# A second block's down projection as seven products with staggered rounds, and its up blocks as 256-column products

## The reference

```
u   = rms_norm(h, norm_mlp_pre)                    # 256 x 1024
hid = square(relu(u @ w_up))                       # 256 x 4096
m   = hid @ w_down                                 # w_down is 4096 x 1024
out = h + rms_norm(m, norm_mlp_post)
```

## Time and profile before

| what | value |
|---|---|
| median of three runs | 1020.5 us |
| the profiled execution, span from first to last instruction | 1018.8 us |
| PE busy | 1010.3 us, 99% of the span |
| DVE busy | 758.5 us, 74% |
| ACT busy | 556.8 us, 55% |
| POOL busy | 232.6 us, 23%; two one-column powers are all it does from 821 us to the end |
| granted TensorE clock, mean | 0.998 |

### The profile page before, as it was taken

The page is one execution under the profiler, slowest core; times in us unless marked ns, Lnnn a source line. Parts: engine busy times, 40 slices in busy tenths (PEclk is TensorE's granted clock), DMA queues, the critical chain, the costliest instruction groups (busy, mean ns, idle before and its releaser), DMA issues.

```text
span 1018.8 us, 14751 instructions
## 1 busy us (share of the span) xinstructions
PE 1010.3 (99%) x5688; PEld 851.1 (84%) x5688; DVE 758.5 (74%) x1208; ACT 556.8 (55%) x848; POOL 232.6 (23%) x322
## 2 busy tenths in 40 slices
PE   9999999999999999999999999999999999999997
PEld 6877788888888877788888888998888888888886
DVE  6997568788777887578787778888865457766665
ACT  6575566545556466656554556845544455334433
POOL 0572600000000272800000004019947620000000
PEclk9999999999999999999999999999999999999999
DMA  9641545555554351365554544553445556564541
GB/s 362 232 159 59 176 155 207 190 182 207 194 180 173 114 218 42 125 221 193 212 195 177 207 168 163 171 201 119 170 150 184 204 186 227 191 214 174 182 149 41
DMA packets 27894, 180.24 MB, mean 177 GB/s; under 512 B 3120, under 2 KB 3248, under 8 KB 7472
## 3 DMA queue, kind: packets, MB, share of 16 engines
q1 hardware_dynamic: 27824, 179.30, 49.5%
HBM read 178.24 MB, written 1.05 MB: 176 GB/s over the span
## 4 chain that ended last, share of the span: by engine, by line
PE 97%; DVE 1%; ACT 1%; DMA 0%; issue 0%; SPq 0%; DVEq 0%
PE pb L747 17%; PE pb L752 10%; PE pb L609 9%; PE pb L610 9%; PE pb L612 8%; PE pb L772 6%; PE pb L771 6%; PE pb L773 6%; PE pb L754 3%; PE pb L1017 2%; PE pb L970 2%; PE pb L673 1%; PE pb L672 1%; PE pb L674 1%; PE pb L709 1%; PE pb L985 1%
## 5 line engine op out<-in xcount | busy, mean ns | idle before, releaser
L1895 DVE TENSOR_TENSOR wlo<-raw,whi 128x2048 fp32r<-128x2048 f32 (+1 forms) x125 | 282.8, 2265 | 102.4 <-ACT whi L1374 102.2
L1374 ACT ACTIVATE whi<-raw 128x2048 fp32r<-128x2048 f32 x159 | 298.5, 1881 | 60.5 <-PE pb L612 34.6
L2772 POOL TENSOR_TENSOR wlo<-raw,whi 128x256 fp32r<-128x256 f32 x268 | 206.8, 810 | 318.9 <-ACT whi L1374 315.2
L747 PE MATMUL pb<-hb,whi 128*128 128x512 f32 x770 | 183.7, 389 | 0.0
L747 PEld LDWEIGHTS pb<-hb,whi 128*128 128x128 f32 x770 | 144.6, 188 | 30.4
L609 PE MATMUL pb<-whi,hb 128*128 128x512 f32 x336 | 134.2, 399 | 0.1
L610 PE MATMUL pb<-wlo,hb 128*128 128x512 f32 x336 | 130.9, 390 | 0.0
L612 PE MATMUL pb<-whi,hb 128*128 128x512 f32 x320 | 124.9, 390 | 0.0
L752 PEld LDWEIGHTS pb<-hb,wlo 128*128 128x128 f32 x880 | 112.8, 191 | 4.3
L752 PE MATMUL pb<-hb,wlo 128*128 128x256 f32 x880 | 114.2, 283 | 0.0
L772 PE MATMUL pb<-wlo,gh 128*128 128x512 f32 x280 | 109.2, 390 | 0.0
(11 more groups left out here) (404 smaller groups left out, 1558.8 us busy)
## 6 DMA issues: line engine op xcount, KB each, us to landing
raw<-wst SPq DMA_DIRECT2D x159, 1024.0 KB, 4.8
raw<-wst SPq DMA_DIRECT2D x10, 512.0 KB, 4.3
gb<-gains SPq DMA_DIRECT2D x3, 512.0 KB, 6.4
XN<-xt SPq DMA_DIRECT2D x2, 512.0 KB, 5.3
X<-x SPq DMA_DIRECT2D x1, 1024.0 KB, 12.1
out<-X SPq DMA_DIRECT2D x4, 256.0 KB, 2.0
PQ<-prm SPq DMA_DIRECT2D x1, 909.0 KB, 4.5
raw<-wst SPq DMA_DIRECT2D x2, 256.0 KB, 7.3
```

Source lines behind the costliest of these rows:

```text
L747: e.matmul(b[:, :], wh[:, k, s], hb2[:, k, :, :].rearrange("p i q -> p (i q)"), start=k == 0, stop=False)
L1374: e.activation(whi[:, split_slot(m), 0:w], raw[:, m % RAW, 0:w], ACT.Copy).then_inc(*hi(m))
L1895: e.tensor_tensor(wlo[:, split_slot(m), s], raw[:, m % RAW, s], whi[:, split_slot(m), s].bitcast(F32), ALU.subtract).then_inc(*lo_v(m))
L2772: g = e.tensor_tensor(wlo[:, split_slot(m), s], raw[:, m % RAW, s], whi[:, split_slot(m), s].bitcast(F32), ALU.subtract)
```

## The change

The down projection of every round is made of seven block products where there were eight, after Winograd's form of Strassen's method. The 256 tokens, the 256 hidden features and the 1024 output columns of a round are each cut in two, so that `hid` and `w_down` become 2 x 2 blocks. Products 1, 2 and 4 take blocks of `hid` and of `w_down` (with one exception: the block of product 4 is replaced by the sum that GpSimd leaves in `raw`); products 3, 5, 6 and 7 take sums of blocks. Each product is 3 matmuls (high and low parts) of 512 columns and has a PSUM bank of its own over all rounds, so a round has 21 matmuls where it had 24, and the output is put together from the seven banks once, at the end.

The sums are new work. GpSimd (`weight_sums`) makes three sums of w_down's blocks in `sums_at`, and a fourth in place in `raw`: four steps of 512 columns in pieces of 256, eight instructions. VectorE makes the sums of hidden blocks, `token_sums` (512 columns, in three instructions). All sums need high and low parts: ACT makes `shared_high` (1536 columns) and `tokens_high` (512), VectorE the low parts of 1024 columns and of `tokens_low`, GpSimd the low part of the last 512 columns in two pieces.

The up blocks are 24 matmuls of 256 columns each (`narrow_block`), which all add into the same 256 columns of one bank. ACT takes them out with relu (`evict`), and VectorE only squares them; the reduce over the two halves is gone. The first round's up blocks stay as they were.

The rounds are staggered: after round j's first up block TensorE takes products 3, 5, 6 and 7 of round j - 2, after its second up block products 1, 2 and 4 of round j - 1. The up tiles now alternate between two split buffers, even down tiles have a third, and odd ones one of their own; these and the sums lie in memory that earlier stages used.

```diff
+            def narrow_block(j, i):
+                m = ups[j]
+                wh, wl = (w.rearrange("p (k c) -> p k c", k=8) for w in parts(m))
+                s, b = slice(128 * i, 128 * i + 128), up_half(j, i)
+                q.wait_ge(*hi[m])
+                bank_free(up_bank(j, i))
+                for k in range(8):
+                    e.matmul(b, wh[:, k, s], hh[:, k, :], start=k == 0, stop=False)
+                    e.matmul(b, wh[:, k, s], hl[:, k, :], start=False, stop=False)
+                q.wait_ge(*lo_of(m)[m])
+                for k in range(8):
+                    mm = e.matmul(b, wl[:, k, s], hh[:, k, :], start=False, stop=k == 7)
+                mm.then_inc(*(used(m) if i else half_used(m)))
...
+            def quarter_products(j, *names):
...
+                for n in names:
+                    if n in (1, 2, 4):
+                        weights_ready(m)
+                        q.wait_ge(*gl_done[m])
+                    else:
+                        q.wait_ge(*tokens_lo[j])
+                    if n in (5, 6):
+                        q.wait_ge(*sums_lo[j])
+                    if n == 7:
+                        q.wait_ge(*sums_lo_g[j])
...
+                    o, (high, low, w_high, w_low) = PB[b][:, :], pair[n]
+                    e.matmul(o, high, w_high, start=j == 0, stop=False)
+                    e.matmul(o, high, w_low, start=False, stop=False)
+                    mm = e.matmul(o, low, w_high, start=False, stop=j == 15)
...
-                for j in range(16):
-                    b = 2 * (j % 2)
-                    if j:
-                        wide(tile_at[2, "up", j, 0], (b, b + 1), lp)
-                    else:
-                        wide_by_k(tile_at[2, "up", 0, 0], (0, 1), lp, [hh_done[("lp", 2), "column", k] for k in range(8)])
...
+                for j in range(1, 16):
+                    narrow_block(j, 0)
+                    free[up_bank(j, 0)] = ff_low[2, j, 0]
+                    if j > 1:
+                        quarter_products(j - 2, 3, 5, 6, 7)
+                    narrow_block(j, 1)
+                    free[up_bank(j, 1)] = ff_low[2, j, 1]
+                    quarter_products(j - 1, 1, 2, 4)
+                quarter_products(14, 3, 5, 6, 7)
+                quarter_products(15, 1, 2, 4, 6, 7, 5, 3)
...
+                def quarters_high(j):
+                    q.wait_ge(*summed_w[j])
+                    q.wait_ge(*used[slot_before(downs[j])])
+                    e.activation(parts(downs[j])[0], raw[:, downs[j] % RAW, :], ACT.Copy).then_inc(*hi(downs[j]))
+                def sums_high(j):
+                    q.wait_ge(*summed_w[j])
+                    q.wait_ge(*(used[downs[13]] if j == 15 else used[downs[j - 1]] if j else used[last_out]))
+                    e.activation(sums_parts(j)[0], sums_at[j % 2], ACT.Copy).then_inc(*sums_hi(j))
...
+                for j in range(16):
+                    if j > 1:
+                        quarters_high(j - 1)
+                    evict(j, 0)
                     if j:
-                        ahead(2, "down", j - 1, 0)
-                ahead(2, "down", 15, 0)
-                for t in range(2):
-                    for c in range(2):
-                        post_square("post2", t, c, lambda t, n: last_down(2, t, n))
+                        features_high(j - 1)
+                    if j == 15:
+                        quarters_high(15)
+                    if j:
+                        sums_high(j - 1)
+                    evict(j, 1)
+                    if j < 14:
+                        split(ups[j + 2])
...
+                def hidden_and_sums(j):
...
+                        e.tensor_tensor(z, both[:, :, 0, :], both[:, :, 0, :], ALU.mult).then_inc(*ff_glu(2, j))
...
+                    e.tensor_tensor(ts[:, 0:2, :], g[:, 0:2, :], g[:, 1:4:2, :], ALU.subtract).then_inc(*dve())
+                    q.wait_ge(*q.prev)
+                    e.tensor_tensor(ts[:, 2, :], ts[:, 0, :], g[:, 3, :], ALU.add).then_inc(*dve())
+                    q.wait_ge(*q.prev)
+                    e.tensor_tensor(ts[:, 3, :], ts[:, 2, :], g[:, 2, :], ALU.subtract).then_inc(*tokens_sum(j))
...
+                    if 0 < j < 15:
+                        split(ups[j + 1])
+                    if j > 1:
+                        split(downs[j - 1])
                     if j:
-                        ahead(2, "down", j - 1, 0)
-                ahead(2, "down", 15, 0)
-                for t in range(2):
...
+                        features_low(j - 1)
...
+                    if j:
+                        sums_low(j - 1)
+                    hidden_and_sums(j)
...
+            def weight_sums(j):
+                r, o = raw[:, downs[j] % RAW, :], sums_at[j % 2]
+                q.wait_ge(*landed(downs[j]))
+                if j >= 2:
+                    q.wait_ge(*sums_lo[j - 2])
+                    q.wait_ge(*sums_lo_g[j - 2])
+                def pieces(dst, a, b, op):
+                    for c in range(0, 512, PIECE):
+                        g = e.tensor_tensor(dst[:, c:c + PIECE], a[:, c:c + PIECE], b[:, c:c + PIECE], op)
+                    return g
+                pieces(o[:, 0:512], r[:, 1024:1536], r[:, 0:512], ALU.subtract).then_inc(*pool())
+                pieces(o[:, 1024:1536], r[:, 1536:2048], r[:, 1024:1536], ALU.add)
+                q.wait_ge(*q.prev)
+                pieces(o[:, 512:1024], r[:, 1536:2048], o[:, 0:512], ALU.add).then_inc(*pool())
+                q.wait_ge(*q.prev)
+                pieces(r[:, 1024:1536], o[:, 512:1024], r[:, 512:1024], ALU.subtract).then_inc(*summed_w(j))
+            def sums_low(j):
+                high, low = sums_parts(j)
+                q.wait_ge(*sums_hi[j])
+                for c in range(1024, 1536, PIECE):
+                    s = slice(c, c + PIECE)
+                    g = e.tensor_tensor(low[:, s], sums_at[j % 2][:, s], high[:, s].bitcast(F32), ALU.subtract)
+                g.then_inc(*sums_lo_g(j))
...
+            weight_sums(0)
             root("post1")
-            m = ahead_to(m, 2, "down", 15, 0)
-            root("post2")
+            for j in range(16):
+                if j < 15:
+                    weight_sums(j + 1)
...
+                sums_low(j)
...
+            for t in range(2):
+                post_gain(t)
+            root("post2", (1, 0))
```

More of the change, by code:

```diff
@@ L388, in stacked @@
             return whi[:, split_slot(m), 0:1024].rearrange("p (k i c) -> p k i c", k=8, i=2)
+        ups = [tile_at[2, "up", j, 0] for j in range(16)]
+        downs = [tile_at[2, "down", j, 0] for j in range(16)]
+        last_out = tile_at[2, "out", 1, 1]
+        ODD_SLOT = 3
         def split_slot(m):
+            if m in ups:
+                return nth[ups[ups.index(m) % 2]] % SPL
+            if m == downs[15]:
+                return split_slot(ups[14])
+            if m in downs:
+                return ODD_SLOT if downs.index(m) % 2 else nth[last_out] % SPL
             return nth[m] % SPL
         def slot_before(m):
+            if m in ups[2:]:
+                return ups[ups.index(m) - 2]
+            if m == downs[15]:
+                return ups[14]
+            if m in downs:
+                return downs[downs.index(m) - 2] if downs.index(m) > 1 else last_out
             return order[nth[m] - SPL] if nth[m] >= SPL else None
@@ L515, in squared @@
                 return E[:, 2 + t, :] if h else XN[:, 1, 512 * t:512 * t + 512]
+            if n[0] == "lp":
+                return E[:, 2 + t, :] if h else rl[:, t, :]
             return XN[:, t, 512 * h:512 * h + 512]
@@ L1858, in second_block, with evict @@
                 high_half(n, 1, par2("lp"))
-                for j in range(16):
-                    ahead(2, "up", j, 0)
-                    if j == 0:
-                        square_half(n, 0)
-                        square_half(n, 1)
-                    z = (cc, th)[j % 2][:, :, :]
+                def evict(j, i):
+                    q.wait_ge(*(used if i or not j else half_used)[ups[j]])
+                    if j > 1:
+                        q.wait_ge(*ff_glu[2, j - 2])
+                    elif j:
+                        q.wait_ge(*squares[("lp", 2), 1, 1])
+                    e.activation(E[:, 2 * (j % 2) + i, 0:L if j else 2 * L], up_half(j, i),
+                                 ACT.Relu if j else ACT.Copy).then_inc(*ff_low(2, j, i))
@@ new lines, in second_block @@
+                sums_high(15)
+                features_high(15)
+                q.wait_ge(*product[1])
+                q.wait_ge(*ff_glu[2, 15])
+                e.activation(E[:, 0, :], PB[PRODUCTB[1]][:, :], ACT.Copy).then_inc(*act("first product"))
+                for i, (t, c) in enumerate(((0, 0), (1, 0), (1, 1), (0, 1))):
+                    q.wait_ge(*total[t, c])
+                    e.activation((E[:, 2, :], E[:, 3, :], rl[:, 0, :], rl[:, 1, :])[i], total_at[t, c], ACT.Square, scale=1.0 / 32,
```

(13 more changed lines are left out.)

197 lines of the change are left out of this document (156 added, 41 removed).

## The result

The changed kernel takes 1070.4 us in the median (1069.3 to 1070.8, four runs) beside 1020.5 for the kernel before in the same comparison: a ratio of 1.049, 95% interval 1.047 to 1.050. The prediction was 1067 us. It is slower, by 50 us.

The account below looks back on a forecast made before the run. PE bound the kernel before; VectorE and GpSimd, taking turns at SBUF, would bound the stage after. Span 1018.8 - 8.0 (PE) + 47.6 (waiting) + 4.6 (start) + 2.5 (end) = 1065.5; median 1.7 higher, 1067 us, range 1048 to 1092.

Parts of the forecast that it names:

- PE's own -8.0 us: TensorE's matmul time: down part 24 to 21 matmuls, -10.9 us; up part +2.9; together -8.0, a round of 10.5 us.
- ScalarE hidden: ScalarE's copies and evictions take 7.2 us of a 10.5 us round, hidden under PE's matmuls, 3.3 us from costing anything.
- The steady round, 13.9: Thirteen middle rounds: VectorE and GpSimd taking turns need 13.9 us each, between 13.6 with tight handovers and 15.9 without overlap.
- The tight sum of 13.6: One round's ten GpSimd pieces plus what VectorE's nine instructions add between them, every handover tight: 13.6 us.
- Where PE would wait: PE waits about 3.4 us a round, at the low part `gl` ahead of products 1, 2 and 4.
- No chain closes the round later: In the rounds, ScalarE's 7.2 us, its wait for product 7 (ended some 3 us early) and tile loads never set the pace.
- The start, mark at 853.9: Round 0's `shared_low` starts at 853.9, after a start costing +4.6 us: 1.3 late, 3.3 of PE stalling.
- The last round, 12.8: Last round, without an up tile to split but with 1024 more down-tile columns: 12.8 us, from 1034.6 to 1047.4.
- PE's end, mark + 10.7: From `shared_low` 14's start at 1047.4, product 1 starts 5.9 us later, 21 matmuls need 4.8; PE ends at 1058.1.
- The tail, 7.4: From PE's end to the span's end: 5.3 us as before, plus 2.1 for outputs queuing on VectorE; end at 1065.5.
- the first (no interference, 1016.8): Rival for the rounds: VectorE and GpSimd do not get in each other's way, PE stays the bound, 1016.8 us; chance 0.07.
- The clock did fall: Rival: PE's clock halves in the rounds' gaps, 1170 us if it stayed; falls likely, 0 to 1 us a round; chance 0.03.

Follow-up runs that it names:

- short pieces: The changed kernel with every GpSimd piece in the feed-forward cut from 256 to 8 columns, same order and waits, sums not real: 1018.9 us, ratio 0.999.
- fills: The changed kernel with GpSimd's pieces replaced by memsets of about the same length that read nothing, sums not real: 1020.8 us, ratio 1.000.

## Why the prediction was right, and where it was not

Its forecast, that VectorE and GpSimd take turns and set the round, is shown: the short pieces and the fills take the loss away, moving work off GpSimd gives back 12 and 29 us, and eight such pieces a round are free where they fit. Step by step:

- **PE's own -8.0 us.** Near. With GpSimd out of the way PE's rounds are 10.56 us apart (predicted 10.5, before 11.01). The up blocks cost 3.1 us (predicted 2.9).
- **ScalarE hidden.** Its busy time never set a round, but its place in the order did in the last one.
- **The steady round, 13.9.** Too high by 0.5: 13 rounds of 13.38 give 6.7 us less. The tight sum of 13.6 was the nearer one. It needs only one of the two engines to have its next instruction waiting at all times, and that was GpSimd, idle for 0.24 us a round; VectorE was idle for 10.4 us in the twelve steady rounds. That VectorE's idle time adds nothing to a round in which GpSimd never stops is argued from these rows. Where PE would wait was wrong: mostly at product 7, not at `gl`. So was "No chain closes the round later": ScalarE waited up to 3.9 us for PE's product 7 before `shared_high`, and VectorE stood idle behind that (3.1 us in two rounds) and behind evictions that waited for PE (4.3 us, two rounds). Single rounds went from 12.4 to 15.1 us where 13.6 to 14.5 were to be seen, and PE was under way for 85% and not 77%, since products at the lower clock take longer.
- **The start, mark at 853.9.** 853.6; PE's stall at `gl` of round 0 was 2.78 us for a predicted 3.3.
- **The last round, 12.8.** This term was mis-sized most: 19.2, +6.4 us. I had counted columns and not the order. ScalarE stands in `quarters_high(15)`, which waits for GpSimd's sums, ahead of `sums_high(14)`, and VectorE behind it:

```profile
1043.49 1.91 ACT L1985 ACTIVATE whi<-raw 128x2048 fp32r<-128x2048 f32 x1 [6.68 <-POOL raw L3008]
1045.31 1.47 ACT L1990 ACTIVATE shared_high<-sums 128x1536 fp32r<-128x1536 f32 x1
```
```profile
1045.43 1.22 DVE L2921 TENSOR_TENSOR wlo<-raw,whi 128x1024 fp32r<-128x1024 f32 x1 [5.46 <-ACT whi L1985]
1046.80 1.23 DVE L2874 TENSOR_TENSOR shared_low<-sums,shared_high 128x1024 fp32r<-128x1024 f32 x1
```

- **PE's end, mark + 10.7.** +13.1. Product 1 starts 6.0 us behind the mark (predicted 5.9); the 21 matmuls from there on take 7.1 us for 4.8. After the 4.4 us stall PE's clock was down: the first ten of the 21 start 0.43 us apart, the others 0.227. The row is the stretch from the mark to the end of PE, the clock third from last, and below it stand the first of the 21 and the eleventh:

```profile
1046.80:1060.00 13.20, 11.34 (x30) 8.21 (x30) 11.14 (x12) 4.20 (x7) 10.64 (x10) 0.61 0.01 1
```
```profile
1052.81 0.77 PE L861 MATMUL pb<-whi,gh 128*128 128x512 f32 x1 [0.52 <-DVE gl L2903]
...
1057.22 0.46 PE L862 MATMUL pb<-odd_low,mg 128*128 128x512 f32 x1
```

- **The tail, 7.4.** 9.3. It is 9.3 in the kernel with short pieces too, so GpSimd's column work has no part in it. Four additions to X stand behind the last root where the earlier trace rows had two, 1.3 us that I left out; the other 0.6 is spread over the outputs.

```profile
1063.79 2.74 DVE L2960 SCALAR_TENSOR_TENSOR X<-XN,sm,X 128x512 f32<-128x512 f32 x4 [0.31 <-POOL sm L3038]
```

Added up: -0.3 - 6.7 + 6.4 + 2.4 + 1.9 = +3.7, the way from the predicted span of 1065.5 to 1069.2. So the total is nearer than its terms deserve, and that is luck: two errors of over 6 us cancel.

Of the rivals, the first (no interference, 1016.8) is what the short pieces bring about, 1018.9; its condition does not hold for this kernel. The clock did fall, eight times in the stage, and came back each time. In the steady rounds it cost nothing that I can see, since GpSimd was under way throughout; it did lengthen the up blocks that VectorE then waited for. Its price at the end is above. No run changed the clock alone, so that these 2.4 us are the clock's is argued from the pace of the products and not shown by an experiment, and the same holds for the steady rounds.

## What to carry to other kernels

Before moving work to an idle GpSimd, take its time and add what each VectorE instruction with two operands in SBUF adds between two pieces (2.04 us for 2048 columns, 0.44 for 512, from the earlier trace rows), and compare the sum with the round of the engine that bounds. At 10.6 us under a round of 11.0 the move was free; at 13.6 the round became 13.4 to 13.5. The plain sum of all durations, 11.6 and 15.9, is too high in both cases. In this kernel, where it did not fit, the work was better on VectorE, which needs 0.6 us for 512 columns where two pieces on GpSimd take 1.06 from VectorE's time. The whole change took PE's round from 11.01 to 10.56 us, so it could pay for no more than 0.45 us a round of waiting. And write out the last round by itself: it came out 6.4 us longer than predicted, though putting its order right gave back only 2.9.

## What I had not expected of the hardware

- The stretch of a VectorE instruction is proportional to the columns of the piece: for 512 columns 0.69 us alone, and 0.94, 1.22 and 1.79 beside pieces of 128, 256 and 512: 0.25, 0.53 and 1.10 us, 2.0 to 2.15 ns a column. I find no price of the handover itself. From 512 to 2048 columns of its own it makes no difference; the token sums, short and each waiting for the one before, are stretched less, from 0.43 to 0.78 us (256 columns) and from 0.29 to 0.72 (128).
- One piece goes between two VectorE instructions, so the count of pieces matters: twenty pieces of 128 in place of ten of 256 cost 22 us more, with the same columns.
- Even pieces of 8 columns are held: in the kernel with short pieces two of them took 4.34 us beside VectorE's 2048-column instructions, which kept their 2.29.

```profile
905.73 4.50 DVE L2045 TENSOR_TENSOR wlo<-raw,whi 128x2048 fp32r<-128x2048 f32 x2
```
```profile
905.95 4.34 POOL L3008 TENSOR_TENSOR raw<-sums,raw 128x8 f32<-128x8 f32 x2
```
